# A second table of expert sums in a mixture-of-experts block

## What is computed

```
x  = x + gate1 * mix(x)                        # attention and pooling
h2 = modulate(rmsnorm(x, norm2_g), shift2, scale2)
# routing: 8 of 128 experts per token, weights wts; rows sorted into blocks of 128 of one expert
def expert_block(tok, rw, e):
    xs = h2[tok]                               # gather
    y = (silu(xs @ w_gate_e[e]) * (xs @ w_up_e[e])) @ w_down_e[e]
    return y * rw[:, None]
routed = zeros(T + 1, D).at[row_tok].add(y)    # add at the tokens' rows
x  = x + gate2 * (routed + shared(h2))
out = rmsnorm(x, final_g)
```

## Time and profile before

| | |
|---|---|
| runs | 3518.12, 3520.7, 3538.77 us; median 3520.7 us |
| profiled execution | span 3472.9 us from the first to the last instruction; its own time is not given apart from the runs, whose median is 47.8 us above the span |
| tiles | 122 to 925 us |
| block table | 925 to 992 us |
| expert blocks | 992 to 3426 us, 11.3 us for each of 215 |
| read back, normalise, store | 3426 to 3473 us |
| busy over the span | PE 85%, VectorE 62%, ScalarE 49%, GpSimd 27% |

### The profile page before, as it was taken

The page is one execution under the profiler, slowest core; times in us unless marked ns, Lnnn a source line. Parts: engine busy times, 40 slices in busy tenths (PEclk is TensorE's granted clock), DMA queues, the critical chain, the costliest instruction groups (busy, mean ns, idle before and its releaser), DMA issues.

```text
span 3472.9 us, 61999 instructions
## 1 busy us (share of the span) xinstructions
PE 2951.9 (85%) x13151; PEld 2180.6 (63%) x13152; DVE 2164.1 (62%) x3443; ACT 1706.3 (49%) x2435; POOL 925.5 (27%) x794
## 2 busy tenths in 40 slices
PE   6699999999469989888798888888888888998883
PEld 2355555555358877776676767676767667776662
DVE  1146666666643665667676766666766675667774
ACT  0133333333133654656565655556556565656565
POOL 0001111111223333232333333333332323333331
PEclk9899999999779999999899999999999999999896
DMA  9501111111175887989998999899989998899997
GB/s 368 163 25 49 49 48 36 49 36 43 67 182 122 239 228 208 269 260 259 289 295 252 290 281 274 258 271 285 288 259 265 265 293 232 247 266 280 294 275 249
DMA packets 415300, 730.08 MB, mean 210 GB/s; under 512 B 31521, under 2 KB 297377, under 8 KB 414754
## 3 DMA queue, kind: packets, MB, share of 16 engines
q1 hardware_dynamic: 341314, 500.17, 42.5%
q0 software_dynamic: 73824, 228.47, 28.6%
HBM read 587.37 MB, written 141.19 MB: 210 GB/s over the span
## 4 chain that ended last, share of the span: by engine, by line
DMA 45%; PE 22%; issue 12%; DVE 8%; POOL 7%; POOLq 4%; ACT 2%; DVEq 0%; SPq 0%; ACTq 0%
DMA rec<-rec_tab 42%; PE PB L986 8%; POOL arena L461 3%; POOL acc_tab L492 3%; POOLq L476 3%; PE PB L951 2%; PE PB L1068 2%; PE PB L1070 2%; PE PB L1069 2%; DMA arena<-in_ada_b 1%; PE PB L1045 1%; PE PB L956 1%; DMA acc_tab<-arena,rec 1%; PE PB L970 1%; PE PB L1011 1%
## 5 line engine op out<-in xcount | busy, mean ns | idle before, releaser
L887 DVE TENSOR_TENSOR WS<-RAW,WS (+1 forms) x774 | 900.8, 1219 | 127.3 <-ACT WS L586 125.3
L586 ACT CAST WS<-RAW (+1 forms) x774 | 759.5, 1052 | 153.2 <-DMA RAW<-in_w_up_e 99.6
L1068 PE MATMUL PB<-WS,XR 128*128 x1720 | 685.6, 399 | 52.2 <-issue 46.6
L461 POOL DMA_INDIRECT arena<-h_tab,rec x219 | 255.3, 1166 | 1574.7 <-DMA rec<-rec_tab 1381.1
L1070 PE MATMUL PB<-WS,XR 128*128 x1720 | 674.7, 392 | 0.0
L1069 PE MATMUL PB<-WS,XR 128*128 x1720 | 674.0, 392 | 0.0
L917 DVE SCALAR_TENSOR_TENSOR arena<-PB,rec,G 128x512 f32<-128x512 f32 x430 | 302.5, 745 | 383.7 <-DMA acc_tab<-arena,rec 336.5
L1068 PE MATMUL PB<-WS,HR 128*128 x860 | 402.9, 468 | 154.1 <-DVE HR L921 153.0
L492 POOL DMA_INDIRECT acc_tab<-arena,rec x215 | 402.5, 1872 | 93.3 <-issue 68.4
L1068 PEld LDWEIGHTS PB<-WS,XR 128*128 128x128 f32 x1720 | 327.6, 190 | 158.7 <-issue 91.8
L1069 PEld LDWEIGHTS PB<-WS,XR 128*128 128x128 f32 x1720 | 326.7, 190 | 66.1
(11 more groups left out here) (233 smaller groups left out, 2982.6 us busy)
## 6 DMA issues: line engine op xcount, KB each, us to landing
RAW<-in_w_gate_e SPq DMA_DIRECT2D x128, 1024.0 KB
RAW<-in_w_up_e SPq DMA_DIRECT2D x128, 1024.0 KB
RAW<-in_w_down_e SPq DMA_DIRECT2D x128, 1024.0 KB, 8.6
arena<-in_ada_w SPq DMA_DIRECT2D x12, 2048.0 KB, 14.3
arena<-in_x SPq DMA_DIRECT2D x32, 512.0 KB, 3.6
h_tab<-arena SPq DMA_DIRECT2D x17, 512.0 KB, 2.9
acc_tab<-arena SPq DMA_DIRECT2D x16, 512.0 KB, 2.6
out<-fa SPq DMA_DIRECT2D x16, 512.0 KB, 4.7
```

Source lines behind the costliest of these rows:

```text
L461: g.indirect_dma_start(xg[n % AHEAD], None, h2_tab, bass.IndirectOffsetOnAxis(ap=rec[:, n % UNROLL, 0:1], axis=0)).then_inc(s[f"xg_r{n % A ...
L586: nc.scalar.copy(to, of).then_inc(s["a_hig" if k < 4 else "a_hid"], 1)
L887: last = V.tensor_tensor(lo, raw, hi, ALU.subtract)
L1068: mm(bank, hi[:, k, :], w(k, 0), start=(k == 0), stop=False)
```

## The change

There are two tables, `acc_tab` and a new `acc2_tab`. Scatters of blocks with even number go to the first with the semaphore `added0`, those with odd number to the second with `added1`, and a scatter waits for the one before it in its own table. The second table is cleared by SyncE, a 512 KB write in each tile and one for the padding rows, from a piece of zeros that VectorE fills before the tiles; GpSimd waits for these (`z_acc`) before its loop. VectorE computes how many blocks are even and odd, GpSimd waits for both counts at the end. There, GpSimd adds each group of `acc2_tab` onto `fa` by an accumulating DMA once the group's load is in, and ScalarE waits for that (`f_sum`). VectorE gets one more semaphore mark in each block.

```diff
--- before.py
+++ after.py
@@ -122,6 +122,8 @@
 
         h2_tab = nc.dram_tensor("h2_tab", [T + P, D], f32).ap()
         acc_tab = nc.dram_tensor("acc_tab", [T + P, D], f32).ap()
+        acc2_tab = nc.dram_tensor("acc2_tab", [T + P, D], f32).ap()
+        accs = (acc_tab, acc2_tab)
         rec_tab = nc.dram_tensor("rec_tab", [(E + 1) * T, 2], i32).ap()
         row_tab = nc.dram_tensor("row_tab", [NTABS * P], i32).ap()
 
@@ -204,6 +206,7 @@
         gains = S[:, 1024:3072].rearrange("p (a n) -> p a n", a=2)
         pad_rec = S[:, 3072:5120].bitcast(i32)
         zeros = S[:, 5120:6144]
+        zeros2 = W[:, 18432:19456]
 
         smallc = sb("smallc", [P, 256])
         col = lambda n, w=1: smallc[:, n:n + w]
@@ -224,7 +227,7 @@
         offi = sb("offi", [P, NTABS], i32)
 
         tab = cst[0:1, AT["band0"][0]:AT["band0"][0] + (NTABS + 1) * P].bitcast(i32)
-        nblk_i = sb("nblk_i", [1, 2], i32)
+        nblk_i = sb("nblk_i", [1, 4], i32)
         rec = sb("rec", [P, UNROLL, 2], i32)
         recf = rec[:, :, :].bitcast(f32)
 
@@ -237,8 +240,8 @@
             v_cb v_mod v_trig v_wo v_x1 v_sub v_v1 v_v2 v_h2 v_P v_rank v_recs v_rope v_mx v_PT v_yT v_mask v_xn v_ch v_c16
             s_xin s_xres st_x1 st_h2 st_rec
             e_cnt e_nb e_off e_tab e_row e_thr
-            w_gu w_dn a_hig a_hid v_spg v_spd rec_ld xg_r0 xg_r1 xg_r2 xg_r3 xg_used gu_done eg_done h_ready hT_a hT_sb xgT_a xgT_v y_done y_v added
-            f_in0 f_in1 f_in2 f_in3 f_in4 f_sq f_v f_ln f_y f_out f_st f_g f_go f_ch""".split()
+            w_gu w_dn a_hig a_hid v_spg v_spd rec_ld xg_r0 xg_r1 xg_r2 xg_r3 xg_used gu_done eg_done h_ready hT_a hT_sb xgT_a xgT_v y_done y_v added0 added1
+            z_acc v_z2 f_in0 f_in1 f_in2 f_in3 f_in4 f_sum0 f_sum1 f_sum2 f_sum3 f_sum4 f_sq f_v f_ln f_y f_out f_st f_g f_go f_ch""".split()
         s = {n: sem(n) for n in names}
 
         def W8(eng, name, val):
@@ -360,8 +363,13 @@
                 if ok(i):
                     W8(sp, "st_x1", 16 * i)
                     sp.dma_start(xres, rows(A["x"][0], i)).then_inc(s["s_xres"], 16)
+                    if isinstance(i, int) and i == 0:
+                        sp.wait_ge(s["v_z2"], 1)
+                    sp.dma_start(rows(acc2_tab, i), zeros2).then_inc(s["z_acc"], 16)
 
             tiles(sp, step)
+            sp.wait_ge(s["v_z2"], 1)
+            sp.dma_start(acc2_tab[T:T + P, :], zeros2).then_inc(s["z_acc"], 16)
 
             def load(m, slot, part):
 
@@ -439,7 +447,7 @@
             g.wait_ge(s["z_dve"], 1)
             for n in range(2):
                 at = T + n * (P // 2)
-                g.dma_start(acc_tab[at:at + P // 2, :], zeros[0:P // 2, :]).then_inc(s["added"], 16)
+                g.dma_start(acc_tab[at:at + P // 2, :], zeros[0:P // 2, :]).then_inc(s[f"added{n}"], 16)
 
             def step(i):
                 if ok(i - 2):
@@ -470,6 +478,7 @@
             g.wait_ge(s["e_tab"], 16)
             g.wait_ge(s["e_thr"], 1)
             g.wait_ge(s["st_x1"], 16 * NT)
+            g.wait_ge(s["z_acc"], 16 * (NT + 1))
             nblk = g.value_load(nblk_i[0:1, 0:1], min_val=NT + 1, max_val=NT + 255)
 
             def load_rec(b, slot):
@@ -486,16 +495,23 @@
                             g.wait_ge(s["rec_ld"], b * 16 + 16 * (AHEAD + 2))
                             gather(n + AHEAD)
                             g.wait_ge(s["y_v"], b + 2)
-
-                            g.wait_ge(s["added"], b * 16 + 32)
+                            g.wait_ge(s[f"added{n % 2}"], q * (8 * UNROLL) + 16 * (n // 2 + 1))
                             settle(g)
-                            g.indirect_dma_start(acc_tab, bass.IndirectOffsetOnAxis(ap=rec[:, (n - 1) % UNROLL, 0:1], axis=0),
-                                                 ys[(n - 1) % 2], None, compute_op=ALU.add).then_inc(s["added"], 16)
+                            g.indirect_dma_start(accs[n % 2], bass.IndirectOffsetOnAxis(ap=rec[:, (n - 1) % UNROLL, 0:1], axis=0),
+                                                 ys[(n - 1) % 2], None, compute_op=ALU.add).then_inc(s[f"added{n % 2}"], 16)
                             load_rec(b + (AHEAD + 2), (n + AHEAD + 2) % UNROLL)
                     settle(g)
-            g.wait_ge(s["added"], nblk * 16 + 48)
+            nb0 = g.value_load(nblk_i[0:1, 2:3], min_val=1, max_val=(NT + 256) // 2)
+            nb1 = g.value_load(nblk_i[0:1, 3:4], min_val=1, max_val=(NT + 256) // 2)
+            g.wait_ge(s["added0"], nb0 * 16 + 16)
+            settle(g)
+            g.wait_ge(s["added1"], nb1 * 16 + 16)
+            settle(g)
             g.wait_ge(s["rec_ld"], nblk * 16 + 16 * (AHEAD + 3))
             g.sem_inc(s["f_go"], 1)
+            for n, (lo, hi) in enumerate(groups):
+                g.wait_ge(s[f"f_in{n}"], 16)
+                g.dma_start(fa[:, lo:hi, :], acc2_tab[lo * P:hi * P, :].rearrange("(t p) n -> p t n", p=P), accum_op=ALU.add).then_inc(s[f"f_sum{n}"], 16)
 
 
         @block.scalar
@@ -623,7 +639,7 @@
 
 
             for n, (lo, hi) in enumerate(groups):
-                act.wait_ge(s[f"f_in{n}"], 16)
+                act.wait_ge(s[f"f_sum{n}"], 16)
                 for t in range(lo, hi):
                     A_(fsq[:, t, :], fa[:, t, :], ACT.Square, accum_out=fss[:, t:t + 1]).then_inc(s["f_sq"], 1)
                 act.wait_ge(s["f_v"], n + 1)
@@ -687,7 +703,9 @@
             link(V.scalar_tensor_tensor(out=A2, in0=A2, scalar=1.0, in1=gains[:, 1, :], op0=ALU.add, op1=ALU.mult))
             v.wait_ge(s["z_fill"], 48)
             v.wait_ge(s["st_h2"], 16)
-            v.wait_ge(s["added"], 32)
+            v.wait_ge(s["added0"], 16)
+            v.wait_ge(s["added1"], 16)
+            V.memset(zeros2, 0.0).then_inc(s["v_z2"], 1)
             V.memset(uP, 0.0)
             V.memset(vE, 0.0)
             V.memset(kb, 0.0)
@@ -830,6 +848,12 @@
             V.tensor_scalar(cumb, B[6][:, P:2 * P], float(NT), None, ALU.add)
             link(V.tensor_copy(cumn, B[6][:, 2 * P:3 * P]))
             V.tensor_copy(nblk_i[:, 0:1], cumb[0:1, E - 1:E])
+            link(V.tensor_scalar(gs[0:1, 6:7], cumb[0:1, E - 1:E], 0.5, 0.75, ALU.mult, ALU.add))
+            link(V.tensor_scalar(gs[0:1, 6:7], gs[0:1, 6:7], 12582912.0, None, ALU.add))
+            link(V.tensor_scalar(gs[0:1, 6:7], gs[0:1, 6:7], -12582912.0, None, ALU.add))
+            link(V.tensor_tensor(gs[0:1, 7:8], cumb[0:1, E - 1:E], gs[0:1, 6:7], ALU.subtract))
+            V.tensor_copy(nblk_i[:, 2:3], gs[0:1, 6:7])
+            V.tensor_scalar(nblk_i[:, 3:4], gs[0:1, 7:8], 1.0, None, ALU.add)
             nl = gs[:, 5:6]
             link(V.tensor_scalar(nl, cumn[:, E - 1:E], 1.0, None, ALU.add))
             V.tensor_copy(nblk_i[:, 1:2], nl[0:1, :])
@@ -911,7 +935,8 @@
                             with v.If(mg > 0):
                                 lower(mg, range(4), "v_spg")
                             v.wait_ge(s["y_done"], b + 1)
-                            v.wait_ge(s["added"], b * 16 + 16)
+                            v.wait_ge(s[f"added{n % 2}"], q * (8 * UNROLL) + 16 * (n // 2 + 1))
+                            settle(v)
 
                             for c in range(2):
                                 last = V.scalar_tensor_tensor(out=ys[(n - 1) % 2][:, c * 512:(c + 1) * 512], in0=B[4 + c], scalar=recf[:, (n - 1) % UNROLL, 1:2],
```

## The result

The changed kernel takes 3597.06 us (median of three, 3591.59 to 3598.93) against 3520.7 us: a ratio of 1.0202, 95% interval 1.0151 to 1.0253. Between the medians that is +76 us where +51 was forecast, 1 us beyond the upper end of the range; the ratio times 3520.7 is 3592 us, +71, inside it. Ratios leave out executions over 1.5% above the fastest of their kernel, so they can differ from the quotient of the medians. Two more comparisons on other chips gave 1.0140 (0.9995 to 1.0285) and 1.0129 (1.0074 to 1.0184), which are +50 and +46 us of 3549 and 3562, with the medians 21 and 41 us apart: by the second, the closer one, the change costs about 1.3%.

The account below looks back on a forecast made before the run. It took GpSimd's queue, waiting for record loads behind scatters, to bound the blocks, and DMA the end. Terms 48 + 1.2 + 0.9 + 0.9 = +51 us gave a 3524 us span, plus 47.8 to the median: 3572 us, range 3541 to 3596.

Parts of the forecast that it names:

- What bounds the blocks: Expert blocks: the chain runs through GpSimd's queue, where the gather waits 1381.1 us for the record load behind the scatter.
- part 1: Line 490, the scatter waits for the one two blocks back: worth at most 28.9 us, taken as 0.
- the count at line 914: VectorE's wait guarding buffer `ys`: it needs the same scatter, b-2, before and after, so this wait stays.
- Rival A: Blocks: the relaxed wait pays its bound, all 28.9 us come back, 3543 us; chance 5%.
- rival B: Blocks: scatters of two tables run faster, 193 instead of 159 GB/s, 125 us gained, 3447 us; chance 8%.
- Part 3: Tiles: 17 clears of 512 KB from SyncE's queue, 44 us without cover, taken as 0.
- Parts 2, 4 and 5: VectorE's extra mark per block +1.2 us, memset of zeros +0.9, six small instructions for the block counts +0.9.
- Part 6, the rate: Final addition in the last stage: accumulating 8.39 MB runs at 193 GB/s, 43.5 us.
- Rival C: Last stage: accumulating into SBUF costs only the plain rate, +28 us in all, 3549 us; chance 12%.
- the fit of the Trainium skill: Last stage: 2.0 us plus bytes/436e3 us per GpSimd transfer, so the five additions take 29 us at most.
- Rival D: Last stage: new transfers don't overlap, descriptors (20 us) or loads in sequence, +57 to +68 and 3, 3581 to 3592 us; 13%.
- Part 6, the end of the stage: Last stage: loads, accumulations and ten tiles' stores (13 us), then 13.1 us from group 3's scaling to the end: +48 us.

Follow-up runs that it names:

- a_noadd: The changed kernel without the final addition of the second table, odd blocks' sums left out of the result: 3504.48 us, ratio 1.0026 to the kernel before.
- b_clear: The kernel before plus only the memset of zeros, the 17 clears from SyncE's queue and GpSimd's wait for them: 3496.48 us, ratio 0.9994.
- a_poolclear: The changed kernel with the 17 clears issued by GpSimd in one burst before the tiles: 3534.9 us, ratio 1.0112 to the kernel before.

## Why the prediction came out as it did

- **What bounds the blocks, part 1, the count at line 914: right.** The record load ends last, the relaxed wait never did. a_noadd agrees: no gain without the final addition. Rival A (28.9 us) and rival B (faster scatters of two tables) are out: blocks of 2424 to 2448 us with two tables, 2420 to 2449 with one.
- **Part 3, the clears: right**, by b_clear (-2 us, -9 to +5). I sized the transfer at 2.6 us; each landed in 5.2 us, issued right behind the tile's load, without effect.
- **Parts 2, 4 and 5**: +3 forecast, +9 (2 to 16) measured together with parts 1 and 3 in a_noadd; not told apart, and +3 is not excluded.
- **Part 6, the rate: right.** 199 GB/s into SBUF against 193 taken from an accumulation into HBM. Rival C, and the estimate by the fit of the Trainium skill ("DMA: Bandwidth & Descriptors", anatomy of one DMA, SWDGE path), are refuted by this row: 42.1 us of work, not 21 to 29. Rival D is out as well: the stage grew by 39.2 us, not by 57 to 68, though the median of 3597 us alone would speak for it.
- **Part 6, the end of the stage: the mis-sized term.** I put the stores of ten tiles ahead of the last accumulation and 13 us of scaling and stores with idle DMA engines behind it: +48. Measured is +39.2. Group 3 landed 64.7 us after the stage's start, not 73.2, and the last group 72.1, not 79; 4.85 MB of stores, nine tiles and not six, were left after it. Stores and additions share the engines, so stores waited (14.3 us to landing at the median, 4.7 before) and filled the end. The stage is as long as its work, 43.9 + 42.1 = 86.0 us, and summing the work would have given 41.4 + 43.5 = 85. That this comes within 1 us is in part luck, as the two shares overlap and the same sum for the kernel before has 41.4 us for a stage of 46.6.
- **Sum:** 39 + 9 = +48 us by the experiments, against +51; whole kernels gave +39 (a_poolclear, 29 to 49), +46 and +50. So close a sum is partly luck: the last stage was put 9 us too high and the rest, as measured, 6 us too low. The two medians say +76. Their three runs each, and 58 us in the tiles of the two profiles, leave room for executions of different length; that this is the reason is likely but not shown, as only one execution of each is profiled.
- **The base of the sum: wrongly read, without effect.** "47.8 us above it" was carried over as what separates a run from its span. That is 1.7 us in every run that has both; the rest is the quickness of one execution. The forecast does not hang on it, as 3524 + 47.8 is the same as the 51 us added to the median of 3520.7.

## What to carry to other kernels

Before relaxing a wait, look at which wait of the queue ends last, and whether the DMA that it waits for can be issued earlier: here moving one small load from behind the block's scatter to ahead of it brought 4.6%, and the second table, which took away the visible dependence, brought nothing and cost a pass over 8 MB. In a stage that the DMA engines fill, add up the transfers' work before laying out a path; an accumulating transfer counted double here. And hold a profile's span against its own run's time before carrying a sum over to a median.

## What was not expected of the hardware

- The tiles' stage takes 693 to 699 us in some executions and 745 to 767 us in others, by chip more than by kernel: all four profiles of one chip were short, all seven of two others long, and with them went the kernel before, 3485 to 3512 us at a mean granted clock of 0.934 to 0.944 on the first, 3501 to 3584 us at 0.928 to 0.944 on the others. The pair shown first has one of each.
- GpSimd's instruction for an addition of 256 or 512 rows took 1.18 to 1.29 us, about as long as a record load of 128 rows (1.22 us); nothing is left of the 9.5 ns a row behind rival D's 20 us.
- An accumulating DMA into SBUF ran at 199 GB/s, the one into HBM at 193, plain ones at 405.
